# A hybrid decoder layer on one core: the hand-over to the value products is split and started earlier, and two modulation vectors move to the vector engine

## The reference, cut to what matters

```
mod = (c_act @ w_ada[l] + b_ada[l])[:, None, :]
sh1, sc1, g1, sh2, sc2, g2 = jnp.split(mod, N_MOD, axis=-1)
h = x * (1.0 + sc1) + sh1
mix = hybrid_mixer(h, ...)            # h @ w_in; attention and SSD; @ w_out
x = layer_norm(ALPHA * x + (1.0 + g1) * mix, ln1_g[l], ln1_b[l])
h = x * (1.0 + sc2) + sh2
...
# peer_ffn: 16 of 16384 experts per head (8 heads), by two lists of 128 keys
u = jnp.take(u_tab, ix, axis=0)
act = gelu(einsum('td,tkd->tk', hx, u))
vv = jnp.take(v_tab, ix, axis=0)
out = einsum('tk,tkd->td', gx * act, vv)
x = layer_norm(ALPHA * x + (1.0 + g2) * out, ln2_g[l], ln2_b[l])
```

## Time and profile before

| | us |
|---|---|
| median of 3 runs | 3328.11 |
| lowest, highest | 3323.17, 3329.9 |
| the profiled execution, its own time | 3327.78 |
| its span, first to last instruction | 3326.0 |

### The profile page before, as it was taken

One profiled execution on the slowest core, in us unless ns is written; L12 is line 12 of the kernel. 1 busy time (PEld: TensorE's weight loads), 2 busy tenths in 40 slices (PEclk: granted clock), 3 DMA queues, 4 the chain that ended last, 5 costly groups with the idle time before them and its releaser, 6 DMA issues.

```text
span 3326.0 us, 44344 instructions
## 1 busy us (share of the span) xinstructions
PE 3159.8 (95%) x16336; PEld 2672.9 (80%) x16336; DVE 2387.9 (72%) x3424; ACT 1060.7 (32%) x1619; POOL 1033.7 (31%) x734
## 2 busy tenths in 40 slices
PE   6999999999799999997999999999999999999994
PEld 3776887666449999996777799999999999999983
DVE  2342564743809999994888877888888888888857
ACT  1323455421303334332232233232333332333232
POOL 0110000000006635533222323435555555545300
PEclk9999999999899999998999999999999999999997
DMA  9776113465034455466888888889899989998753
GB/s 356 276 274 221 58 57 140 165 236 182 26 125 150 148 186 175 161 207 215 288 291 289 272 280 283 302 297 343 313 335 333 343 306 337 339 329 307 285 186 120
DMA packets 277263, 792.99 MB, mean 238 GB/s; under 512 B 118224, under 2 KB 138880, under 8 KB 230784
## 3 DMA queue, kind: packets, MB, share of 16 engines
q1 hardware_dynamic: 219648, 463.74, 41.5%
q0 software_dynamic: 50560, 317.87, 25.3%
q10 hardware_dynamic: 6912, 9.44, 0.8%
HBM read 747.97 MB, written 43.00 MB: 238 GB/s over the span
## 4 chain that ended last, share of the span: by engine, by line
PE 78%; DVE 14%; DMA 3%; issue 2%; ACT 1%; SPq 1%; POOL 0%; DVEq 0%; ACTq 0%; POOLq 0%
PE ps L2184 27%; PE ps L2122 26%; PE ps L1854 14%; PE ps L2097 3%; DVE arena L1614 3%; PE ps L1819 2%; PE ps L1878 1%; DVE arena L1640 1%; DVE arena L1611 1%; DVE split L1714 1%; PE ps L2143 1%; PE ps L1793 1%; PE ps L1913 1%; DMA arena<-in_w_ada 1%; DVE arena L1346 1%
## 5 line engine op out<-in xcount | busy, mean ns | idle before, releaser
L2184 PE MATMUL ps<-split,w_parts 128*128 128x512 f32 x4608 | 1074.0, 393 | 37.0 <-DVE split L1714 34.2
L2184 PEld LDWEIGHTS ps<-split,w_parts 128*128 128x128 f32 x4608 | 865.3, 189 | 235.4 <-DVE split L1714 35.5
L2122 PE MATMUL ps<-h_parts,split 128*128 128x384 f32 x5376 | 947.5, 335 | 1.1 <-DVE split L1714 1.1
L2122 PEld LDWEIGHTS ps<-h_parts,split 128*128 128x128 f32 x5376 | 933.6, 188 | 5.0 <-DVE split L1714 1.7
L1111 ACT ACTIVATE split<-below_parts 128x1024 fp32r<-128x1024 f32 x416 | 441.5, 1062 | 1210.3 <-PE ps L2184 702.8
L1714 DVE TENSOR_TENSOR split<-below_parts,split 128x1024 fp32r<-128x1024 f32 x416 | 509.2, 1224 | 276.7 <-ACT split L1111 271.7
L788 POOL COPY arena<-arena 128x1 uint32 x256 | 209.4, 818 | 710.6 <-DVE arena L1664 399.6
L1202 DVE TENSOR_TENSOR win_parts<-arena,win_parts 128x512 fp32r<-128x512 f32 (+2 forms) x208 | 129.2, 630 | 309.8 <-ACT win_parts L841 301.5
L1645 DVE CUSTOM_DVE_ANT_0 arena<-arena 128x2048 f32<-128x2048 f32 x128 | 293.1, 2290 | 14.9 <-DMA arena<-in_u_tab,arena 14.9
L1664 DVE SCALAR_TENSOR_TENSOR arena<-arena 128x2048 f32<-128x2048 f32 x128 | 300.7, 2350 | 2.9 <-DVE arena L1656 2.2
L791 POOL DMA_INDIRECT arena<-in_v_tab,arena x128 | 263.4, 2058 | 104.4 <-POOL arena L788 103.0
(11 more groups left out here) (267 smaller groups left out, 3214.9 us busy)
## 6 DMA issues: line engine op xcount, KB each, us to landing
below_parts<-in_u_units SPq DMA_DIRECT2D x256, 512.0 KB, 4.9
below_parts<-in_v_tab SPq DMA_DIRECT2D x256, 512.0 KB, 6.9
arena<-in_w_ada SPq DMA_DIRECT2D x96, 1024.0 KB, 7.4
arena<-in_w_slices POOLq DMA_DIRECT2D x56, 512.0 KB, 4.2
gates_by_expert<-arena SPq DMA_DIRECT2D x24, 1024.0 KB, 4.8
below_parts<-gates_by_expert SPq DMA_DIRECT2D x32, 768.0 KB, 9.1
arena<-in_w_out POOLq DMA_DIRECT2D x32, 512.0 KB, 5.0
acts_ahead<-arena ACTq DMA_DIRECT2D x48, 192.0 KB, 2.3
```

The source lines that it names most:

```text
L2122: ins = nc.tensor.matmul(ps[:, 6 + b, 0:DT], lhs[:, cols], h2_parts[:, rhs, k, :], start=k == 0 and n == 0, stop=k == KT - 1 and n == 2)
L2184: ins = nc.tensor.matmul(ps[:, g.bank_of(half, m) + b, :], w_parts[:, buf, lhs, i, m * P:(m + 1) * P], rhs[:, b * 512:(b + 1) * 512], star ...
```

## The change

Four things are done.

- The first two later vectors (32 tiles) are accumulated by VectorE in `acc`, one instruction for a tile (`later_row`), which then waits for its own end; ScalarE's two copies go, and TensorE's sums over partitions are 16 products with a column of ones. `modulated` runs one unit later for all four vectors (beside n = 57, 80, 157, 183).
- ScalarE stages two quads of gates at the start of its turn n and two at its end.
- ScalarE splits the first group's four tiles after half tiles 93, 94, 95 and behind the loop, and makes the high parts of the first two units of `v` at 94 and 95. VectorE runs "start" ahead of the clearing of `out4`, SP reads the gates and activations of "start" inside its loop and the gates of the second group right behind them. TensorE's wait for the last Gelu moves to the third block of its first unit.
- `stage` and the third buffer of early parts move within the memory of `w_parts`: `stage` to its start, the buffer behind it, where the tiles of "start" do not lie.

```diff
 PRE_RAWS, PRE_SPLITS = 4, 3
 EXP_AT, COLS_AT, SC_AT = (12, 28, 53, 77), (19, 43, 67), (3, 19, 45)
 GATES_AT = (34, 58, 82)
+HANDED = EARLY - 1
+TILES_AT = (EARLY - 3, EARLY - 2, EARLY - 1, EARLY)
 BATCHES = 2
...
-STAGE = QZ
-PARTS = 26 * K
+STAGE = PARTS = 26 * K
...
 def stream(engine, group):
 
-    group(Group("start", 0))
     group(Group("ahead", 1))
...
         pre_parts = [split[:, 0, :, :], split[:, 1, :, :],
-                     w_parts.rearrange("p a b c d -> p (a b c d)")[:, 0:2 * UNIT].rearrange("p (a b) -> p a b", a=2)]
-        assert PARTS + 2 * UNIT <= STAGE
+                     w_parts.rearrange("p a b c d -> p (a b c d)")[:, 2 * NKEY * TG:2 * NKEY * TG + 2 * UNIT].rearrange("p (a b) -> p a b", a=2)]
+        assert 2 * NKEY * TG + 2 * UNIT <= WP and 2 * NKEY * TG >= WP // 2
...
+            def read_back(g, i):
+                if not (g.kind == "start" and i < 2):
+                    sp.wait_ge(w_ready, g.val(GT, i - 1))
+                sp.dma_start(gel[:, i % 2, :], acts_out[bass.ds(g.val(GT, i), 1), :, :].rearrange("a p n -> (a p) n"))\
+                    .then_inc(gel_full[i % 2], 16)
+
+            def gates_in(g):
+
+                buf = g.c % 2
+                sp.dma_start(gm[:, buf, :, :], gates_out[:, :, bass.ds(g.val(GT), GT), :].rearrange("p a b c -> p a (b c)"))\
+                    .then_inc(gm_full[buf], 16)
...
-            for i in range(max(EARLY - 6 - GATES_AT[DB - 1], 0), GATES_FOR):
-                store_gates(DB - 1, i)
-            for i in range(2):
-                sp.wait_ge(g_stored[i], 16 * (DT // TG // 2))
-                sp.wait_ge(acts_stored[i], 16 * (GT // 2))
+                if n == HANDED:
+                    for i in range(2):
+                        sp.wait_ge(g_stored[i], 16 * (DT // TG // 2))
+                        sp.wait_ge(acts_stored[i], 16 * GT)
+                    gates_in(Group("start", 0))
+                    for i in range(2):
+                        read_back(Group("start", 0), i)
+            for i in range(2, GT):
+                read_back(Group("start", 0), i)
+            gates_in(Group("ahead", 1))
             sp.wait_ge(x1_moved, 16)
...
-                if g.second:
-                    for i in range(2):
-                        sp.wait_ge(acts_stored[i], 16 * (AHEAD * GT // 2))
...
-                if g.kind != "last":
-                    if not (g.kind == "start" or g.second):
-                        sp.wait_ge(w_made, g.val(GT, -GT))
-                    buf = g.c % 2
-                    sp.dma_start(gm[:, buf, :, :], gates_out[:, :, bass.ds(g.val(GT), GT), :].rearrange("p a b c -> p a (b c)"))\
-                        .then_inc(gm_full[buf], 16)
-                if g.kind == "start":
-                    for i in range(GT):
-                        read_back(g, i)
+                if not (g.second or g.kind == "last"):
+                    sp.wait_ge(w_made, g.val(GT, -GT))
+                    gates_in(g)
...
+                if g.second:
+                    for i in range(2):
+                        sp.wait_ge(acts_stored[i], 16 * (AHEAD * GT // 2))
...
-                if n + 1 in SUMS_AT:
+                if SUMS_AT.get(n + 1, 0) >= 2:
                     i = SUMS_AT[n + 1]
                     act.wait_ge(ada_used, 2 * KT + (i + 1) * KT)
-                    nc.scalar.activation((acc if i < 2 else later_acc)[:, 0:512], ps[:, 7, :], ACT.Copy).then_inc(ada_row, 1)
+                    nc.scalar.activation(later_acc[:, 0:512], ps[:, 7, :], ACT.Copy).then_inc(ada_row, 1)
...
-            def gates_staged(m, i):
+            def gates_staged(m, i, quads):
...
-                for q in range(TG // 4):
+                for q in quads:
...
+            def tile_high(g, i):
+
+                act.wait_ge(w_made, g.val(GT, i + 1))
+                nc.scalar.activation(w_parts[:, g.c % 2, 0, i, :], gel[:, i % 2, :], ACT.Copy).then_inc(w_high, 1)
+
+            def unit_high(g, j):
+
+                act.wait_ge(raw_full[j % RAWS], g.unit(0) * 4 + (16 * (j // RAWS + 1)))
+                if g.second and j < 2:
+                    act.wait_ge(pre_used, EARLY - 2 + j)
+                else:
+                    act.wait_ge(unit_used, g.unit(j - 1))
+                nc.scalar.activation(split[:, j % 2, 0, :], raw[:, j % RAWS, :], ACT.Copy).then_inc(high_done, 1)
+
             for n in range(EARLY):
+                for m in range(DB):
+                    if 0 <= n - GATES_AT[m] < GATES_FOR:
+                        gates_staged(m, n - GATES_AT[m], (0, 1))
                 if n + PRE_SPLITS < EARLY:
                     early_high(n + PRE_SPLITS)
+                if n >= EARLY - 2:
+                    unit_high(Group("ahead", 1), n - (EARLY - 2))
                 if n % 2:
                     early_gelu(n // 2)
...
-                        gates_staged(m, n - GATES_AT[m])
+                        gates_staged(m, n - GATES_AT[m], (2, 3))
+                if n in TILES_AT:
+                    tile_high(Group("start", 0), TILES_AT.index(n))
+            tile_high(Group("start", 0), GT - 1)
...
+            def later_row(n):
+
+                i, k, tile = n // KT, n % KT, 2 * KT + n
+                what = ada[:, n % 4, :]
+                dve.wait_ge(ada_full[n % 4], 16 * (2 * KT // ADAS + n // 4 + 1))
+                if k == 0:
+                    dve.wait_ge(mod_sum, CHUNKS + i)
+                    ins = nc.vector.tensor_scalar(acc, what, c_act[:, k:k + 1], None, ALU.mult)
+                else:
+                    ins = nc.vector.scalar_tensor_tensor(acc, what, c_act[:, k:k + 1], acc, ALU.mult, ALU.add)
+                ins.then_inc(ada_used, 1)
+                dve.wait_ge(ada_used, tile + 1)
...
-                if n in SUMS_AT:
-                    modulated(SUMS_AT[n])
+                if LATER_AT.get(n, 2 * KT) < 2 * KT:
+                    later_row(LATER_AT[n])
+                if n - 1 in SUMS_AT:
+                    modulated(SUMS_AT[n - 1])
...
-            own(nc.vector.memset(out4, 0.0))
...
+            group(Group("start", 0))
+            own(nc.vector.memset(out4, 0.0))
             stream(dve, group)
...
-                from_acc = acc if i < 2 else later_acc
-                pe.wait_ge(ada_row, 2 * CHUNKS + i + 1)
+                if i < 2:
+                    pe.wait_ge(ada_used, 2 * KT + (i + 1) * KT)
+                    pe.wait_ge(mod_ready, CHUNKS + i)
+                else:
+                    pe.wait_ge(ada_row, 2 * CHUNKS + i - 1)
                 for k in range(KT):
                     a, part = k // GROUPED, slice(k % GROUPED * P, (k % GROUPED + 1) * P)
-                    ins = nc.tensor.matmul(ps[:, 7, k:k + 1], from_acc[:, part], ident[:, 32 * a:32 * a + 1], start=True, stop=True)
+                    if i < 2:
+                        ins = nc.tensor.matmul(ps[:, 7, k:k + 1], acc[:, k * P:(k + 1) * P], ones[:, 0:1], start=True, stop=True)
+                    else:
+                        ins = nc.tensor.matmul(ps[:, 7, k:k + 1], later_acc[:, part], ident[:, 32 * a:32 * a + 1], start=True, stop=True)
...
-                if n in LATER_AT:
+                if LATER_AT.get(n, 0) >= 2 * KT:
...
+                            if g.second and j == 0 and m == 2:
+                                pe.wait_ge(pre_gelu, AHEAD * GT)
...
-            pe.wait_ge(pre_gelu, AHEAD * GT)
```

More of the change, by code:

```diff
@@ L670, in _ @@
                         sp.dma_start(raw[:, j, :], v_tiles[j, :, 0:UNIT]).then_inc(raw_full[j], 16)
-            for i in range(max(EARLY - 6 - GATES_AT[DB - 1], 0), GATES_FOR):
-                store_gates(DB - 1, i)
-            for i in range(2):
-                sp.wait_ge(g_stored[i], 16 * (DT // TG // 2))
-                sp.wait_ge(acts_stored[i], 16 * (GT // 2))
-            sp.wait_ge(x1_moved, 16)
[L678 to L682, removed]
+                if n == HANDED:
[8 more added lines that the diff above has]
+            gates_in(Group("ahead", 1))
+            sp.wait_ge(x1_moved, 16)
             def group(g):
-                if g.second:
-                    for i in range(2):
-                        sp.wait_ge(acts_stored[i], 16 * (AHEAD * GT // 2))
                 if g.kind == "full" and g.p is None and g.c == GROUPS - 1:
@@ L1100, in _ @@
                     if 0 <= n - GATES_AT[m] < GATES_FOR:
-                        gates_staged(m, n - GATES_AT[m])
+                        gates_staged(m, n - GATES_AT[m], (2, 3))
+                if n in TILES_AT:
+                    tile_high(Group("start", 0), TILES_AT.index(n))
+            tile_high(Group("start", 0), GT - 1)
             def group(g):
-                buf = g.c % 2
                 for j in g.steps():
[L1107 to L1111, removed]
+                    if not (g.second and j < 2):
+                        unit_high(g, j)
                     if j == (3 if g.second else 0) and g.sums():
@@ L1122, in group @@
                         if due == "high":
```

(12 more changed lines are left out.)

## The result

| | before | after |
|---|---|---|
| median of 5 runs, us | 3328.11 (3323.17 to 3330.68) | 3303.91 (3299.68 to 3311.07) |
| span of the profiled run, us | 3326.0 | 3302.2 |
| after to before | | 0.9929, 95% interval 0.9914 to 0.9945 |

The account below looks back on a forecast made before the run. TensorE was taken as the bound (78% of the chain of waits), VectorE taking its place in steps 33 to 56. Terms -16.5 + 6 - 4 - 10 = -24.5 gave 3303.5 us; range 3292 to 3317.

Parts of the forecast that it names:

- Term 1: First projections: two vectors' accumulation moves from TensorE to VectorE, which becomes the bound in steps 33 to 56; -16.5 us.
- Term 3: Gate blocks: splitting the quads ends TensorE's pauses at odd half tiles, but VectorE bounds; -4 us (0 to -7).
- what goes: First projections: TensorE loses 32 tiles at 0.99 us each, 31.7 us.
- The rival in which GpSimd's issues are held up: First projections, apparently the slower case: accumulation takes 4.26 us a tile as GpSimd's work meets it; 3346 us, chance 0.03.
- Term 2: Unit 183: TensorE waits for the fourth vector's bias, now behind four banks; +6 us (3.9 to 8).
- The longer pause at half tile 82: Gates, third block: time won in the first two blocks becomes a longer wait for the first one-hot tiles; no size given.
- Its chain does not get shorter: Gate blocks: VectorE, never idle there, keeps its chain's length, so at most 4.1 us come out.
- Term 4: Hand-over to the value groups: second idle and its clock loss go, first product starts 2.4 us later; -10 us (-4 to -13).
- The second idle: Hand-over, ahead of unit 1: TensorE's wait of 9.42 us for a low part goes, with 3.0 us of clock loss.
- The first idle: Hand-over, ahead of the first value product: one idle of 11 to 12 us, with the clearing of `out4` in it.
- The rival of the first gather: Hand-over: the first dot waits for its gathered rows and holds up unit 1; 3309 us, chance 0.10.
- Given back: Later groups: a shift meets their waits for loads of `v` otherwise, so the edits bring nothing net; 3325 us, chance 0.04.

Follow-up runs that it names:

- e_quads: The kernel before with only the four quads of gates split in two and two, ahead of the high part; 0.9984 of the kernel before.
- e_clear: The changed kernel with `out4` cleared ahead of the first value group's splits instead of behind them; 0.9901 of the kernel before.
- e_same: The changed kernel run again, unaltered, for a second trace; 0.9925 of the kernel before.
- e_hand: The kernel before with only the hand-over changed: first value group's tiles, high parts, reads and the clearing of `out4`; 0.9974 of the kernel before.

## Why the prediction was right

The forecast was 0.4 us off, but that is partly luck: the four terms measured -27.2 where -24.5 was forecast, and the other three stretches added 3.4 in this execution. The mechanisms of the terms hold; two sizes inside term 1 and one step of term 3 do not.

- *Term 1, -16.5.* Measured -17.8, -17.4 alone. The mechanism held step by step: VectorE the bound in steps 33 to 56, a stop of 4.84 us at the first sums (5 forecast), low parts late by 4.1 us in all. The step "what goes" was too small, 31.7 for 36.4, because I read the tile's own 0.99 and not the slower start of the unit behind it, which stood in the chain. In steps 33 to 56 it did no harm, as VectorE bounds there: the first sums begin 5.6 us earlier, 5.3 forecast. Behind them TensorE bounds for the most part, and from the first to the second sums 17.4 us came out where 4 + 10.9 - 1.4 = 13.5 was forecast. The clock took that back: start to start the two sums took 6.85 and 5.30 us for 3.49 and 3.46, 5.2 more, where 2 was put down. Two errors of 3 to 4 us nearly cancelled. The rival in which GpSimd's issues are held up is out: 528 ns each. The Trainium skill (SBUF — State Buffer, "SBUF: two separate sides") tells of descriptor writing that stops under VectorE instructions in a two-port mode, and lets an instruction with two inputs in SBUF hold up GpSimd only where GpSimd reads SBUF. The accumulation has two inputs, so the prediction applied the rule too widely; the trace shows no effect on direct loads.
- *Term 2, +6.* Measured +5.6, an idle of 5.57 as forecast, and taken back by one edit.
- *Term 3, -4.* Measured -6.5 to -6.9, at the end of its range. TensorE's waits in the three blocks fell from 14.0 to 8.4 us, and 16 products at the lower clock (2.99 us for 2.02) went. The longer pause at half tile 82 that was to show it did not come: 2.50 us before, twice 1.14 after, as TensorE now waits for VectorE a little in nearly every half tile of the second block too. The tail behind the last one-hot tile shortened by 4.0 in e_quads (26.8 to 22.8 us), which is the step as forecast. The other 2.9 are VectorE's own chain: from the first one-hot tile to the last it took 356.7 us for 359.6, with as many instructions, whose busy time fell from 231.8 to 227.9. "Its chain does not get shorter" was the step that failed. That its tiles met fewer of GpSimd's splits fits, but no run isolated it.
- *Term 4, -10.* Measured -8.5 to -9.0. The second idle went as forecast. The first idle is 13.53, not 11.9: the clearing was taken at its row, 6.88 us, and costs 8.5. The rival of the first gather did not show in the changed kernel, where the first dot starts at once behind the made tile; e_clear shows it.
- *Given back* (rival, 0.04). 5.6 + 2.0 us more in the groups behind. e_same had 4.4 less there with no edit, and e_hand 0.9 less than before, so I take this as the spread of single executions; what makes the spread stays open.

## What to carry to other kernels

When work is moved to an engine with room on average, add up that engine's instructions over the densest stretch: here 16 of the 32 moved tiles brought 2.5 us and the other 16 brought 15.3. Before a filler such as a clearing is taken out of an idle stretch, look at what else it covers; and when a step is delayed by one slot, check each of its instances, as one of four can sit ahead of a long neighbour. And take a second trace of the same kernel before explaining a difference in a stretch that no edit touches: here such stretches spread over 7 to 11 us in twelve traces, and one moved by 4.4 us between two traces of one kernel.

## What the runs showed of the hardware

- *A large clearing costs more than its record.* After, VectorE's last low part ended by 1494.61, then came 1.66 us without a record, the MEMSET of 6.88, and the next instruction at once. 1.66 + 6.88 = 8.54 us for 8192 elements. The same 1.66 stands in all six traces in which the clearing follows a low part. The Trainium skill (VectorE: DVE Perf Modes, "Zero memsets can be issued as uint32 (trn2)") says that a memset takes one cycle per element; at the 0.96 GHz that this page gives for VectorE the estimate is 8.53, and the trace agrees if the gap ahead of the record is counted in. Taking the clearing out of the way shortened TensorE's idle by 8.67.
- *The granted clock differs between executions of the same work.* The stretch from the second sums to unit 183 took 471, 475 or 479 us with mean granted clocks of 0.98, 0.97 and 0.96, for the same instructions and 16.1 to 17.1 us of idle time in the three windows shown.
- *Products of 32 output rows slow what follows them.* The unit behind each tile (four such products, x8 in the row) takes 0.15 to 0.2 us more than one behind a unit: 2.39 for 2.20, 2.94 for 2.75.
- *An issue can block its queue.* One read-back of activations by SP took 6.07 us to issue where the ones before and behind it took 0.33 and 0.59; the load behind it was issued only then and landed 7.87 us later. It is one case in the traces shown, and what held it up is open.
